# Nineteen instead of sixteen pairs of expert chunks per layer take seven products in the second expert product, a transfer finishes two of their four weight sums, and their steps are spread over ten chunks

## The reference

```python
u = jnp.take(expert_down, idx, axis=0)
act = jax.nn.gelu(jnp.einsum('btd,bthkd->bthk', xi, u).astype(jnp.float32))
v_sel = jnp.take(expert_up, idx, axis=0)
return jnp.einsum('bthk,bthkd->btd', (g * act).astype(xi.dtype), v_sel)
```

## Time and profile before

| | us |
|---|---|
| median of 3 runs (2058.97 to 2059.98) | 2059.28 |
| the profiled execution | 2062.64 |
| its span, first to last instruction | 2060.8 |
| busy in it: TensorE / VectorE / ScalarE / GpSimd | 2041.9 / 1639.6 / 1356.2 / 373.4 |
| the second expert product of layer 0, from its first matmul to its last | about 575 to 914 |
| the same of layer 1 | about 1461 to 1799 |

### The profile page before, as it was taken

The page is one execution under the profiler, slowest core; times in us unless marked ns, Lnnn a source line. Parts: engine busy times, 40 slices in busy tenths (PEclk is TensorE's granted clock), DMA queues, the critical chain, the costliest instruction groups (busy, mean ns, idle before and its releaser), DMA issues.

```text
span 2060.8 us, 31647 instructions
## 1 busy us (share of the span) xinstructions
PE 2041.9 (99%) x11776; PEld 1748.3 (85%) x11776; DVE 1639.6 (80%) x2971; ACT 1356.2 (66%) x2303; POOL 373.4 (18%) x183
## 2 busy tenths in 40 slices
PE   8999999999999999999999999999999999999998
PEld 7788988888888888887888888888888888888888
DVE  7968988889868999877589888899689999743456
ACT  6665688878756666666646888777566666544674
POOL 1448800000000000012378100000000000045341
PEclk9999999999999999999999999999999999999999
DMA  6455855555555556664457655555556666676444
GB/s 231 154 155 169 235 174 169 173 166 166 172 188 200 194 195 215 207 202 149 126 170 222 189 171 165 174 165 169 185 188 214 203 195 203 211 217 198 128 157 137
DMA packets 108461, 376.26 MB, mean 183 GB/s; under 512 B 12372, under 2 KB 17908, under 8 KB 107412
## 3 DMA queue, kind: packets, MB, share of 16 engines
q1 hardware_dynamic: 107444, 369.00, 56.2%
q0 software_dynamic: 864, 5.24, 1.3%
HBM read 367.87 MB, written 1.08 MB: 179 GB/s over the span
## 4 chain that ended last, share of the span: by engine, by line
PE 94%; DVE 4%; ACT 1%; DMA 1%; issue 1%; POOL 0%; SPq 0%; DVEq 0%; ACTq 0%
PE ps L211 29%; PE ps L212 14%; PE ps L205 14%; PE ps L207 14%; PE ps L206 14%; PE ps L1121 3%; DVE WL L192 1%; PE ps L1100 1%; DVE arena L813 1%; DMA raw<-in_l_up_dram 0%; PE ps L1144 0%; DVE arena L810 0%; PE ps L2390 0%; PE ps L2414 0%; PE ps L1147 0%
## 5 line engine op out<-in xcount | busy, mean ns | idle before, releaser
L186 ACT ACTIVATE WH<-raw 128x1024 fp32r<-128x1024 f32 (+1 forms) x680 | 701.6, 1036 | 301.1 <-PE ps L207 193.4
L211 PE MATMUL ps<-X,WH 128*128 128x512 f32 x2528 | 898.4, 399 | 0.1
L212 PE MATMUL ps<-X,WL 128*128 128x256 f32 x2528 | 706.4, 279 | 0.0
L192 DVE TENSOR_TENSOR WL<-raw,WH 128x1024 fp32r<-128x1024 f32 (+1 forms) x554 | 661.9, 1197 | 41.2 <-ACT WH L186 40.8
L198 POOL TENSOR_TENSOR WL<-raw,WH 128x1024 fp32r<-128x1024 f32 x126 | 319.1, 2555 | 1571.5 <-ACT WH L186 1569.4
L211 PEld LDWEIGHTS ps<-X,WH 128*128 128x128 f32 x2528 | 474.5, 188 | 110.7 <-issue 0.6
L212 PEld LDWEIGHTS ps<-X,WL 128*128 128x128 f32 x2528 | 476.9, 189 | 0.1
L205 PE MATMUL ps<-WH,X 128*128 128x512 f32 (+1 forms) x784 | 310.1, 396 | 1.5 <-DVE X L414 0.9
L207 PE MATMUL ps<-WH,X 128*128 128x512 f32 (+1 forms) x784 | 305.3, 389 | 0.0
L206 PE MATMUL ps<-WL,X 128*128 128x512 f32 (+1 forms) x784 | 305.1, 389 | 0.0
L205 PEld LDWEIGHTS ps<-WH,X 128*128 128x128 f32 x784 | 147.5, 188 | 36.0 <-issue 3.5
(11 more groups left out here) (355 smaller groups left out, 2665.0 us busy)
## 6 DMA issues: line engine op xcount, KB each, us to landing
raw<-in_l_down_dram SPq DMA_DIRECT2D x256, 512.0 KB, 3.6
raw<-in_l_up_dram SPq DMA_DIRECT2D x256, 512.0 KB, 4.2
raw<-in_l_wq_dram SPq DMA_DIRECT2D x32, 512.0 KB, 3.6
raw<-in_w_qk_dram SPq DMA_DIRECT2D x24, 512.0 KB, 3.8
raw<-in_w_gates_dram SPq DMA_DIRECT2D x24, 512.0 KB, 3.6
raw<-in_l_nat_dram SPq DMA_DIRECT2D x16, 512.0 KB, 3.3
raw<-in_l_wout_dram SPq DMA_DIRECT2D x16, 512.0 KB, 3.6
raw<-in_l_win_dram SPq DMA_DIRECT2D x16, 512.0 KB, 3.8
```

The costliest lines, as they stand in the source:

```text
L186: a.activation(WH[:, i % NW, 0:w], raw[:, i % NW, 0:w], ACT.Copy).then_inc(w_high, 1)
L192: v.tensor_tensor(WL[:, i % NW, 0:w], raw[:, i % NW, 0:w], WH[:, i % NW, 0:w], ALU.subtract).then_inc(w_low_v, 1)
L211: t.matmul(PS[:, bank, :], w[0], X2[:, k, :, :].rearrange("p w t -> p (w t)"), start=first, stop=False)
L212: return t.matmul(PS[:, bank, 0:256], w[1], X2[:, k, 0, :], start=False, stop=last)
```

## The change

SEVEN gets nineteen pairs per layer, 7, 12, 15, 17, 20, 22, ... 52, 55, which stand two and three apart. The steps of a pair lie otherwise, over ten chunks:
- Two of the four weight sums are finished by a transfer. VectorE makes two sums of 512 columns in turn 2p - 2. ScalarE writes the negative of a weight block (turn 2p - 2) and the negative of a sum (turn 2p - 1) into the places of the other two (`seven_minus`, `scale=-1.0`), and GpSimd issues one transfer, which adds two blocks of `expert_up` from memory to these (512 KB, 256 pieces of 2 KB).
- ScalarE makes the high halves of the sums in turns 2p + 4 and 2p + 5, VectorE the low halves in turns 2p + 5 and 2p + 6, and TensorE takes the four products after chunk 2p + 6. The two sums made by VectorE alone come first, those finished by the transfer second.
- The rows' sums take four operations instead of five and lie in turn 2p - 3, their low half in turn 2p - 1.
- There are two places for the weight sums, two for the split row sums and five for the split activations, which a small planner hands out (`OF_SUM_T`, `OF_S`, `OF_A`); the split store has 20 rows.
- The buffers of both chunks of a pair are loaded anew after the second weight sum, that of chunk 2p also after ScalarE's first negative.
- The closing additions lie one turn later.

The diff, cut to its core:

```diff
-        SEVEN = tuple(range(10, 56, 3))
+        SEVEN = (7, 12, 15, 17, 20, 22, 25, 27, 30, 32, 35, 37, 40, 42, 45, 47, 50, 52, 55)
...
+        V_STEPS = (("weights3", -2, 1), ("weights2", -2, 1), ("rows", -3, 4), ("rows_low", -1, 1),
+                   ("low_second", 5, 1), ("low_first", 6, 1))
+        A_STEPS = (("minus_first", -2, 1), ("minus_second", -1, 1), ("rows_high", -2, 1), ("high_second", 4, 1),
+                   ("high_first", 5, 1))
...
+        SUMS_AT = 6
...
-                s.wait_ge(seven_v, seven_count(l, m, ("weights2", "weights4")[j]))
+                s.wait_ge(seven_v, seven_v_at(l, m, "weights2"))
+                if j == 0:
+                    s.wait_ge(seven_a, seven_a_at(l, m, "minus_first"))
...
-                t.wait_ge(seven_v, seven_count(l, m, "weights_low0"))
-                for n, (bank, part) in enumerate(((1, 1), (2, 3), (3, 2), (6, None))):
-                    if n == 2:
-                        t.wait_ge(seven_v, seven_count(l, m, "weights_low1"))
+                t.wait_ge(seven_v, seven_v_at(l, m, "low_second"))
+                for n, bank, part in ((2, 2, 3), (3, 3, 2), (0, 1, 1), (1, 6, None)):
+                    if n == 0:
+                        t.wait_ge(seven_v, seven_v_at(l, m, "low_first"))
...
-                if c % 2 == 0 and c // 2 - 2 in SEVEN:
-                    seven_sums(c // 2 - 2)
+                if c % 2 == 0 and (c - SUMS_AT) // 2 in SEVEN:
+                    seven_sums((c - SUMS_AT) // 2)
...
+        def seven_minus(a, l, c):
+            for m, p in enumerate(SEVEN):
+                w = sum_t(m)
+                if c == 2 * p + AT["minus_first"]:
...
+                    a.activation(w[:, 0, :], raw[:, i % NW, 0:512], ACT.Copy, scale=-1.0).then_inc(seven_a, 1)
+                if c == 2 * p + AT["minus_second"]:
+                    a.wait_ge(seven_v, seven_v_at(l, m, "weights2"))
+                    a.activation(w[:, 1, :], w[:, 3, :], ACT.Copy, scale=-1.0).then_inc(seven_a, 1)
...
+                if c == 2 * p + AT["high_second"]:
+                    a.wait_ge(seven_done, len(SEVEN) * l + m)
+                    a.activation(HIGH_T[:, 2:4, :], sum_t(m)[:, 2:4, :], ACT.Copy).then_inc(seven_a, 1)
+                if c == 2 * p + AT["high_first"]:
+                    a.wait_ge(early_sum, 16 * (N_SUMS * l + 3 + m + 1))
+                    a.activation(HIGH_T[:, 0:2, :], sum_t(m)[:, 0:2, :], ACT.Copy).then_inc(seven_a, 1)
...
             for c in range(124):
                 high(a, up + c + 3)
+                seven_minus(a, l, c)
                 if c % 2 == 0 and c // 2 not in SEVEN:
                     split_g_scalar(a, l, c // 2 + 1)
                 if c % 2 and c // 2 + 1 in SEVEN:
...
                 low_v(v, up + c + 2)
-                if c // 2 + 1 in SEVEN:
-                    seven_vector(v, l, c)
                 if c % 2 == 0:
-                    split_g_vector(v, l, c // 2 + 1)
-                if c // 2 + 1 not in SEVEN:
-                    seven_vector(v, l, c)
+                    p = c // 2 + 1
+                    if p in SEVEN:
+                        seven_weights3(v, l, SEVEN.index(p))
+                    split_g_vector(v, l, p)
+                    if p in SEVEN:
+                        seven_weights2(v, l, SEVEN.index(p))
+                seven_vector(v, l, c)
...
+                if c - 146 in [2 * p for p in SEVEN]:
...
+                    g.wait_ge(seven_a, seven_a_at(l, m, "minus_second"))
+                    g.wait_ge(early_sum, 16 * (N_SUMS * l + 3 + m))
...
+                    g.dma_start(sum_t(m)[:, 0:2, :], rows, accum_op=ALU.add).then_inc(early_sum, 16)
```

More of the change, by code:

```diff
@@ L93, in build @@
         IOT2 = sb("IOT2", [128, 128, 2], BF16)[:, :, :]
-        with nc.sbuf_tensor("split_t", [128, 6, 512], F32R) as SPLIT:
+        with nc.sbuf_tensor("split_t", [128, 20, 512], F32R) as SPLIT:
             pass
@@ L153, in build, with seven_v_at, seven_a_at @@
         seven_v, seven_a, seven_done = (sem("seven_" + n) for n in ("sums_low", "high", "products"))
[L155 to L162, removed]
+        V_STEPS = (("weights3", -2, 1), ("weights2", -2, 1), ("rows", -3, 4), ("rows_low", -1, 1),
+                   ("low_second", 5, 1), ("low_first", 6, 1))
+        A_STEPS = (("minus_first", -2, 1), ("minus_second", -1, 1), ("rows_high", -2, 1), ("high_second", 4, 1),
+                   ("high_first", 5, 1))
+        AT = {what: at for what, at, _ in V_STEPS + A_STEPS}
+        SUMS_AT = 6
+        V_COUNT, A_COUNT = [{} for _ in SEVEN], [{} for _ in SEVEN]
+        n_v = n_a = 0
+        for c in range(124):
+            for what, at, n in V_STEPS:
+                for m, p in enumerate(SEVEN):
+                    if c == 2 * p + at:
+                        n_v += n
+                        V_COUNT[m][what] = n_v
+            for what, at, n in A_STEPS:
+                for m, p in enumerate(SEVEN):
+                    if c == 2 * p + at:
+                        n_a += n
+                        A_COUNT[m][what] = n_a
+        N_V, N_A, N_SUMS = n_v, n_a + 1, 3 + len(SEVEN)
+        def seven_v_at(l, m, what):
+            return N_V * l + V_COUNT[m][what]
+        def seven_a_at(l, m, what):
+            return N_A * l + A_COUNT[m][what]
         def width(i):
@@ L1341, in split_g_scalar @@
                 a.wait_ge(act_head, N_HEAD * l + N_HEAD)
-            if p in (1, 2):
+            q = before(OF_A, p)
+            if q is None:
                 a.wait_ge(w_used, up)
[L1344 to L1349, removed]
+                a.wait_ge(g_low, 64 * l + A_HOMES[OF_A[p]][1])
+            elif q in SEVEN:
+                a.wait_ge(seven_done, len(SEVEN) * l + SEVEN.index(q) + 1)
+            else:
+                a.wait_ge(w_used, up + 2 * q + 2)
             if HEADS[2 * p + 1]:
@@ L1367, in seven_scalar @@
-            if c == 2 * SEVEN[-1] + 7:
+                if c == 2 * p + AT["rows_high"]:
+                    q = before(OF_S, m)
+                    if q is None:
+                        a.wait_ge(g_low, 64 * l + S_HOMES[OF_S[m]][1])
+                    else:
+                        a.wait_ge(seven_done, len(SEVEN) * l + q + 1)
+                    a.wait_ge(seven_v, seven_v_at(l, m, "rows"))
+                    a.activation(split_s(p)[0], SUM_S[:, 0:4, :].rearrange("p a b -> p (a b)"), ACT.Copy).then_inc(seven_a, 1)
@@ new lines, in seven_rows_low, with seven_weights3 @@
+        def seven_rows_low(v, l, m):
+            v.wait_ge(seven_a, seven_a_at(l, m, "rows_high"))
+            high_s, low_s = split_s(SEVEN[m])
+            v.tensor_tensor(low_s, SUM_S[:, 0:4, :].rearrange("p a b -> p (a b)"), high_s, ALU.subtract).then_inc(seven_v, 1)
+        def seven_weights3(v, l, m):
+            i = bases(l)[2] + 2 * SEVEN[m]
+            v.wait_ge(raw_in[(i + 1) % NW], 16 * ((i + 1) // NW + 1))
+            if before(OF_SUM_T, m) is not None:
+                v.wait_ge(seven_v, seven_v_at(l, before(OF_SUM_T, m), "low_second"))
+            v.tensor_tensor(sum_t(m)[:, 2, :], raw[:, (i + 1) % NW, 512:1024], raw[:, i % NW, 512:1024],
+                            ALU.subtract).then_inc(seven_v, 1)
```

148 lines of the change are left out of this document (78 added, 70 removed).

## The result

| | us |
|---|---|
| kernel before, median of 6 runs | 2059.35 (2058.24 to 2061.79) |
| changed kernel, median of 6 runs | 2173.89 (2165.43 to 2181.62) |
| ratio, 95% interval | 1.0551 (1.0531 to 1.0571) |
| profiled execution of the changed kernel, its span | 2169.29, 2167.5 |
| forecast | 2124 (2098 to 2150) |

The change makes the kernel 5.5% slower. The direction was forecast, the size was not: 115 us instead of 65.

The account below looks back on a forecast made before the run. TensorE bounds, VectorE close behind. Per layer, stops of 32.4 us plus 2.1 after stops less 2.0 saved give 32.5, twice is 65; the median 2059.28 becomes 2124 us, range 2098 to 2150.

Parts of the forecast that it names:

- The transfer: GpSimd's 19 more transfers per layer land in 7.9 us, in time by some 5 us; weight loads left where they are.
- kind B: Seven-product pair with the next two ahead, eight per layer: TensorE stands 1.62 us for the low half of the sums.
- Rival 3: Stops let TensorE's clock fall: 27 places after each of 34 stops at 1.2 GHz, 208 us more, 2332; chance 2%.
- kind A: Seven-product pair with another three ahead, nine per layer: TensorE stands 2.16 us for the low half of the sums.
- Pairs 7 and 12: Pair 7 has three full chunks, 9.51 us, and is in time; pair 12 counts among the stops of 2.16 us.
- After a stop: TensorE's next place is 0.31 us long instead of 0.23; 26 stops x 0.08 = 2.1 us per layer.
- the 18 matmuls: Three more seven-product pairs in each of two layers save 18 matmuls on TensorE, 4.1 us, 2.04 us a layer.
- VectorE's falling share: Sign of being right: VectorE's busy share in the second products' stretches falls from 92% to about 80%.
- closing additions: They come one turn later, six chunks of TensorE work ahead of the end; listed as work that costs nothing.
- Rival 1: TensorE stays fed in the second products and the change brings just its 18 matmuls: 2055.2 us; chance 8%.
- Rival 2: Transfer lands late, from 15 us ScalarE waits in kind B; at 18 us 48 us more, 2172; chance 6%.

Follow-up runs that it names:

- e1: Changed kernel with GpSimd's transfer adding only 8 instead of 512 columns of each of two weight blocks, all waits kept: 2127.32 us, ratio 1.0331.
- e7: Changed kernel with the transfer written plainly over the negated copies instead of added, same bytes and waits: 2182.96 us, ratio 1.0611.
- e9: Changed kernel with each 512 KB transfer made as two of 256 KB, the first started one turn earlier: 2152.66 us, ratio 1.0449.
- e2: Changed kernel with TensorE's stops filled by repeating one product of the sums, 252 more matmuls: 2150.40 us, ratio 1.0441.
- e10: Changed kernel with sums after chunk 2p+7, pair 0's split not waiting, second weight sum before low activations, transfer in two halves: 2055.49 us, ratio 0.9980.
- e8: Changed kernel with sixteen seven-product pairs per layer, from pair 12 on each three apart: 2130.82 us, ratio 1.0352.
- e3: Changed kernel with TensorE taking the four products of the sums after chunk 2p+7 instead of 2p+6: 2067.99 us, ratio 1.0036.

## Why the prediction was wrong in size

**The step that failed is "The transfer".** It costed the transfer's effect on the loads at nothing ("by the rows I leave them where they are") and gave room for it only in the upper bound, as one late load of 0.57 us per walk. Measured, the decisive load of kind B took 5.01 to 6.96 us, at pair 20 6.11, where ScalarE stood for 1.37 us, and kind B stopped for 2.86 and 2.67 us on the mean of each layer instead of 1.62. Taking the bytes away (e1) brings the time to 2127, where the forecast had 2124. That these two agree so closely is partly luck: in e1 the stops are 7 us shorter than forecast, and longer gaps (3.5 us) and the time ahead of pair 0 (3.6 us) make up for it. The Trainium skill (DMA: Bandwidth & Descriptors, section Issuing engines are not separate DMA queues) says that transfers from all engines interleave on the same 16 engines. The forecast quoted this and decided against it; e1, e7 and e9 agree with it. The row that I trusted instead could not speak to the question: no row of before had such a transfer beside these loads. And the diff could have told that both start behind the same weight sum.

**Rival 3 was partly true.** I gave 2% to the stops letting the clock fall, since after 7.7 us without a matmul at the start the clock was 1.00. That was misread. TensorE's time line of the kernel before, at the start:

```profile
7.70 3.74 PE L471 MATMUL ps<-cst,arena 128*128 128x128 f32 x16 [7.70 <-DMA cst<-in_cst_dram]
11.24 2.40 PE L464 MATMUL ps<-cst 128*128 128x128 f32 x12
13.71 0.28 PE L246 MATMUL ps<-X,WH 128*128 128x256 f32 x1
13.83 0.28 PE L247 MATMUL ps<-X,WH 128*128 128x256 f32 x1
```

The matmuls of 128 columns start some 0.21 us apart up to 13.1 us, the last two 0.11 us apart, and those of twice as many columns behind them 0.12 us. So after the 7.7 us without a matmul TensorE did run at its lower level. The trace holds no record of the clock before 13.1 us, and the profile gives 1.00 where it has none. Within the dense stream of the changed kernel, some 80 steps ran at 0.43 us, TensorE's lower level (1.2 in place of 2.4 GHz), 16.0 us more than before, and e2 shows that the stops cause it. But my price for it, 27 slow places after each stop, was far too high: the longest such run had 12, and after the regular stops of kind A (0.49 + 1.38 us) none came. The Trainium skill (TensorE: Matmul & The Clock Gate, section HAM oscillation) warns that matmuls with idle gaps between them can fall to the slow clock again and again; the trace agrees for eleven of its sixteen stops of over 2 us, and shows none behind the other five, among them two of 3.12 and 3.28 us.

**Kind A was right, somewhat too long.** 1.87 us instead of 2.16, as 0.49 + 1.38 instead of 0.62 + 1.54. The helpers' path from the end of chunk 2p + 3 to the second half was 9.48 us (pair 17, 680.27 to 689.75) for a forecast of 9.63: the hand-off from VectorE to TensorE took 0.05 us, not 0.15. The rest was booked twice: the longer first step after the first half is in the walk's time already.

**Kind B's walk was right as well,** 1.40 us for most pairs where no load is late (e1) against 1.62; 0.10 of the difference is again the hand-off.

**Pairs 7 and 12.** Pair 7, forecast in time, stopped for 0.8 us, and pair 12 for 3.2 to 3.3; without the transfer's bytes pair 7 does not stop and pair 12 does so as any of kind A.

**After a stop.** The first step was 0.34 us (686.88 to 687.22), not 0.31, and small gaps came on top: 10.0 us where 4.2 stood.

**Not seen: pair 0.** 1.8 us a layer, from one condition in the diff that widened from pairs 1 and 2 to every pair without a predecessor. I checked where the stops go, not what a rewritten condition now includes.

**Right:** the 18 matmuls; VectorE's falling share (75% from 92%, forecast about 80%), though most of the fall is the stretch that got longer, for in e10, where nothing stops, it is 90%; no cost in the closing additions (from the last matmul of layer 0's second product to the last of layer 1's first 546.6 us, before 546.6). Rival 1 fell, but e10 is that case: a lead of one chunk, pair 0 set free, the weight sum first and the transfer spread out give a ratio of 0.9980, which is the 2055.2 that this rival named. Rival 2 fell: the transfer landed in 8.8 us, against the 13.6 us available; its 256 pieces showed in the issue, 1.21 us on GpSimd.

## What to carry to other kernels

A transfer that is itself in time can still cost: ask which loads are under way with it and whether the bounding engine hangs on one of them, and spread its bytes over the turns before. Where a product is moved against the steps that feed it, count the lead in chunks of the bounding engine: here one chunk, 1.36 or 2.72 us long, decided over some 106 us. Read what a rewritten condition newly includes, not only what it replaces. And hold a clock figure of the page against the steps of the matmuls themselves.

## What the hardware showed that I had not expected

- The granted clock fell within a dense stream after stops of 2.0 to 4.4 us (changed kernel, e7, e8, e9), to 0.91 over 10 us, for up to 12 steps of 0.43 us in the changed kernel; stops of 3.12 and 3.28 us there brought none, and regular stops of 0.49 + 1.38 us every 17.8 us left it at 1.00 (e8).
- Filling the stops with 57.1 us of matmuls made the kernel 23.5 us shorter (e2).
- The same 512 KB without adding landed in 6.2 us instead of 8.8 and were issued in 0.72 us instead of 1.21, and yet made the kernel slower still, a ratio of 1.0611 instead of 1.0551 (e7).
- With the DMA engines at 86% TensorE was never free in e10, while at 71% it stood still in the changed kernel (both from 640 to 720 us). In e3 they were at 83% with ScalarE waiting 57.4 us for loads, and TensorE was free for 1.5 us of the 80: the busy share did not tell, the lead over TensorE did.
